# V as the stationary side of the attention's second product, heads normalised in their transposed form

## The reference

```python
def token_mixers(hn, w_in, sink, q_gain, k_gain, rpb, g_grp, w_out):
    proj = jnp.dot(hn, w_in)
    qa, ka, va, qb, kb, vb, qc, kc, vc = jnp.split(proj, offsets, axis=-1)
    ...
    oa = window_sink_attention(...)    # 8 heads, 2 key heads, |q - k| <= 128, a sink logit per head
    ob = dense_block_attention(...)    # 4 heads, 2 key heads, all 512 keys
    oc = neighbourhood_attention(...)  # 4 heads, a 2-D window with a learned bias
    merged = jnp.concatenate([
        rmsnorm(oa, g_grp[:A_WIDTH]),
        rmsnorm(ob, g_grp[A_WIDTH:A_WIDTH + B_WIDTH]),
        rmsnorm(oc, g_grp[A_WIDTH + B_WIDTH:]),
    ], axis=-1)
    return jnp.dot(merged, w_out)

def encoder_layer(x, c, ...):
    hn = rmsnorm(x, g_mix) * (1 + sc1) + sh1
    x = x + gt1 * token_mixers(hn, ...)
    hn = rmsnorm(x, g_ffn) * (1 + sc2) + sh2
    x = x + gt2 * expert_choice_ffn(hn, ...)
    return x
```

## Time and profile before

| | |
|---|---|
| median of 3 runs | 3015.84 us (3008.33 to 3026.54) |
| the profiled execution | 3007.47 us, its span 3005.6 us |
| PE busy in the span | 2685.9 us, 89% |
| weight loads, VectorE, ACT, POOL busy | 54%, 43%, 27%, 9% |
| mean granted clock of TensorE | 0.935 |
| product with V (L1190), 1664 instructions | 231.3 us |
| transposes of the probabilities (L1178), 832 | 144.7 us |

### The profile page before, as it was taken

One profiled execution on the slowest core, in us unless ns is written; L12 is line 12 of the kernel. 1 busy time (PEld: TensorE's weight loads), 2 busy tenths in 40 slices (PEclk: granted clock), 3 DMA queues, 4 the chain that ended last, 5 costly groups with the idle time before them and its releaser, 6 DMA issues.

```text
span 3005.6 us, 32021 instructions
## 1 busy us (share of the span) xinstructions
PE 2685.9 (89%) x10596; PEld 1636.0 (54%) x10596; DVE 1305.8 (43%) x2602; ACT 813.1 (27%) x1613; POOL 269.9 (9%) x260
## 2 busy tenths in 40 slices
PE   6898987989679999999998899698984999999994
PEld 1265764567545555555524567565773555555552
DVE  0346544555434443433404465355554444433444
ACT  0214333154112222222203154232430222222221
POOL 1002000110000000000000110001100000000001
PEclk9898977999789999999999998799996999999997
DMA  9803013021279999999993110213014899999994
GB/s 296 273 1 112 22 43 102 23 90 43 104 246 342 336 353 336 335 335 333 344 315 70 60 60 36 99 25 112 22 43 168 304 353 338 335 336 335 337 341 170
DMA packets 301870, 595.78 MB, mean 198 GB/s; under 512 B 35934, under 2 KB 36078, under 8 KB 301712
## 3 DMA queue, kind: packets, MB, share of 16 engines
q1 hardware_dynamic: 279936, 514.87, 48.1%
q0 software_dynamic: 16976, 62.46, 7.3%
q10 hardware_dynamic: 4832, 16.85, 1.6%
HBM read 552.48 MB, written 43.78 MB: 198 GB/s over the span
## 4 chain that ended last, share of the span: by engine, by line
PE 78%; DVE 8%; issue 7%; DMA 3%; ACT 3%; POOL 1%; POOLq 0%; ACTq 0%; DVEq 0%; SPq 0%; PEld 0%; PEldq 0%
PE bank L1286 29%; PE bank L1139 5%; PE bank L1190 5%; PE bank L1068 4%; PE bank L1303 4%; PE bank L1305 4%; PE bank L1304 4%; PE bank L1169 4%; PE bank L1216 2%; DMA ring<-in_w_ada 2%; PE bank L1178 2%; PE bank L1218 2%; PE bank L1217 2%; PE bank L1236 2%; PE bank L1135 1%
## 5 line engine op out<-in xcount | busy, mean ns | idle before, releaser
L1286 PE MATMUL bank<-ring,hT 128*128 128x512 f32 x2048 | 895.3, 595 | 7.0 <-DVE hT L959 7.0
L1286 PEld LDWEIGHTS bank<-ring,hT 128*128 128x128 f32 x2048 | 388.4, 191 | 473.2 <-issue 470.6
L988 DVE TENSOR_TENSOR ring_r<-ring,down_hi 128x1024 fp32r<-128x1024 f32 x256 | 293.3, 1219 | 0.0
L982 DVE TENSOR_TENSOR pbuf<-pbuf,bank 128x512 f32<-128x512 f32 x64 | 44.0, 688 | 559.2 <-PE bank L1286 559.2
L633 ACT ACTIVATE down_hi<-ring 128x1024 fp32r<-128x1024 f32 x256 | 248.7, 1045 | 99.9 <-DMA ring<-in_w_down 99.9
L1190 PE MATMUL bank<-V,pbuf 128*128 128x64 f32 x1664 | 231.3, 279 | 40.8 <-ACT pbuf L580 30.6
L1190 PEld LDWEIGHTS bank<-V,pbuf 128*128 128x128 f32 x1664 | 215.7, 199 | 59.3 <-ACT pbuf L580 44.5
L1139 PE MATMUL bank<-ring,hT 128*128 128x512 f32 x512 | 228.3, 601 | 0.0
L1303 PE MATMUL bank<-down_hi,hid_hi 128*128 128x512 f32 x512 | 206.5, 403 | 0.0
L1068 PE MATMUL bank<-ring,silu_c 128*2 128x512 f32 x384 | 177.7, 619 | 27.7 <-DMA ring<-in_w_ada 18.2
L1305 PE MATMUL bank<-down_hi,hid_lo 128*128 128x512 f32 x512 | 200.8, 392 | 0.0
(11 more groups left out here) (177 smaller groups left out, 3326.5 us busy)
## 6 DMA issues: line engine op xcount, KB each, us to landing
ring<-in_w_gate SPq DMA_DIRECT2D x64, 2048.0 KB, 10.7
ring<-in_w_up SPq DMA_DIRECT2D x64, 2048.0 KB, 10.1
ring<-in_w_down SPq DMA_DIRECT2D x64, 2048.0 KB, 14.5
ring<-in_w_ada SPq DMA_DIRECT2D x24, 2048.0 KB, 14.7
ring<-in_w_in SPq DMA_DIRECT2D x16, 2048.0 KB, 16.8
ring<-in_w_out SPq DMA_DIRECT2D x8, 2048.0 KB, 10.1
X<-residual ACTq DMA_DIRECT2D x24, 512.0 KB, 3.3
residual<-X POOLq DMA_DIRECT2D x16, 512.0 KB, 2.9
```

What stands on the lines that cost most here:

```text
L988: dve.tensor_tensor(ring_r[4 + n // 4][:, kk:kk + 2, :], ring[4 + n // 4][:, kk:kk + 2, :], full(down_hi[n // 4][kk // 4][:, kk % 4:kk % 4 ...
L1286: ins = pe.matmul(bank[2 * (n % 2) + half][:, :], hT[j % 2][:, k, :], ring[n][:, k, :], start=(k == 0), stop=(k == KT - 1))
```

## The change

The product with V is turned round. V's 64 columns are the stationary side and the transposed probabilities, 128 queries, move. Two heads of a pair (an even and an odd slot) are issued together in the odd slot's turn, one into partitions 0 to 63 and the other into 64 to 127 of bank 5 or 6. The heads thus come out transposed, with features on partitions and queries in columns, in the order of pairs. On the host, the rows of `w_out` and the entries of `g_grp` are put in that order.

The product stands ahead of the transposes of its slot, and it waits for both copies. It waits for `heads_read` at the first pair of each eight heads.

The normalisation works in that form. ACT squares a bank (`heads_a`, `heads_b`). PE sums the squares over the partitions of each head with a two-column constant as moving side (`sum_a`, `sum_b`), which gives one number per query and head. VectorE forms the group's mean with the squared inverse sums; POOL takes the power; VectorE scales the inverse sums (`scale_a`, `scale_b`). PE then spreads each factor over the head's 64 partitions (`spread_a`, `spread_b`), with the factor's column repeated as the stationary side and the identity moving. ACT copies the result out of bank 7, and VectorE multiplies heads, gain and factors in four pieces (`merged_a`, `merged_b`). Rounding and the rest follow as before. All later side steps come two slots later, `normed_0` and `normed_1` three, and the bank's waits count by a table `SIDE`.

```diff
-C_ID, C_MASKA, C_MASKC, C_ROPE, C_END = 0, 128, 512, 576, 1600
+C_ID, C_MASKA, C_MASKC, C_ROPE, C_HALF, C_END = 0, 128, 512, 576, 1600, 1602
...
-AFTER = [(8, "sink"), (8 + V_LAG, "heads_a"), (9 + V_LAG, "scale_a"), (15 + V_LAG, "heads_b"), (17 + V_LAG, "scale_b"),
-         (20, "merged_0"), (21, "split_0"), (22, "merged_1"), (23, "split_1")]
-AFTER += [(23 + 4 * half + quarter, f"out_{half}{quarter}") for half in range(2) for quarter in range(4)]
-AFTER += [(31, "norm"), (32, "normed"), (33, "normed_0"), (34, "normed_1"), (35, "router_0"), (36, "router_1")]
+AFTER = [(8, "sink"), (11, "heads_a"), (17, "sum_a"), (18, "scale_a"), (19, "spread_a"), (20, "merged_a"), (21, "split_a"),
+         (19, "heads_b"), (22, "sum_b"), (23, "scale_b"), (24, "spread_b"), (25, "merged_b"), (26, "split_b")]
+AFTER += [(25 + 4 * half + quarter, f"out_{half}{quarter}") for half in range(2) for quarter in range(4)]
+AFTER += [(33, "norm"), (34, "normed"), (36, "normed_0"), (37, "normed_1"), (37, "router_0"), (38, "router_1")]
 SLOTS = 16 * (TILES - 1) + AFTER[-1][0] + 1
+def heads(p):
+    if p < 4:
+        return slice(p, p + 5, 4)
+    if p < 6:
+        return slice(p + 4, p + 7, 2)
+    return slice(2 * p, 2 * p + 2, 1)
...
+SIDE_ITEMS = ("sum_a", "spread_a", "sum_b", "spread_b", "out_03", "out_13", "normed_0", "normed_1", "router_1")
+SIDE = {}
+for _kind, _i, _k in schedule():
+    if _kind in SIDE_ITEMS:
+        SIDE[_kind, _i] = len(SIDE) + 1
...
                             act.wait_ge(p_turned, m + 1)
                             if m >= 2:
-                                act.wait_ge(pv_done, m - 1)
+                                act.wait_ge(pv_done, m // 2)
                             act.activation(pbuf[:, 3, 0:n], bank[3][:, 0:n], ACT.Copy).then_inc(pt_by_s, 1)
...
-                    if kind in ("merged_0", "merged_1"):
-                        half = int(kind[-1])
-                        act.wait_ge(side_free, 7 * i + 1 + half)
+                    if kind in ("heads_a", "heads_b"):
+                        half = "ab".index(kind[-1])
+                        act.wait_ge(pv_done, 8 * i + 4 * half + 4)
+                        if half:
+                            act.wait_ge(side_full, SIDE["sum_a", i])
+                        elif i:
+                            act.wait_ge(side_full, SIDE["sum_b", i - 1])
+                        act.activation(squares, bank[5 + half][:, :], ACT.Square).then_inc(squared, 1)
+                    if kind in ("spread_a", "spread_b"):
+                        half = "ab".index(kind[-1])
+                        act.wait_ge(side_full, SIDE[kind, i])
                         if i:
-                            act.wait_ge(side_full, 7 * (i - 1) + 4)
+                            act.wait_ge(heads_read, 2 * i - 1 + half)
+                        act.activation(factors[:, 512 * half:512 * half + 512], bank[7][:, :], ACT.Copy).then_inc(spread, 1)
+                        act.wait_ge(spread, 2 * i + half + 1)
+                        act.sem_inc(side_free, 1)
+                    if kind in ("merged_a", "merged_b"):
+                        half = "ab".index(kind[-1])
+                        act.wait_ge(heads_read, 2 * i + half + 1)
+                        if i:
+                            act.wait_ge(side_full, SIDE["out_13", i - 1])
                         part_h = slice(4 * half, 4 * half + 4)
                         act.activation(merged_hi[:, part_h, :], hT[0][:, part_h, :], ACT.Copy).then_inc(merged_hi_ready, 1)
...
-                        a = kind == "heads_a"
-                        half = 0 if a else 1
+                        half = "ab".index(kind[-1])
+                        cols = slice(8 * half, 8 * half + 8)
                         dve.wait_ge(probs_ready, 16 * i + 8 * half + 8)
-                        if a:
+                        if not half:
                             dve.wait_ge(sink_exp, i + 1)
                             chain.add(dve.tensor_tensor(ssum[:, i % 2, 0:8], ssum[:, i % 2, 0:8], stat[:, 16:24], ALU.add))
-                        chain.add(dve.reciprocal(rinv[:, 8 * half:8 * half + 8], ssum[:, i % 2, 8 * half:8 * half + 8]))
-                        dve.wait_ge(pv_done, 16 * i + 8 * half + 8)
-                        if a and i == 0:
-                            dve.wait_ge(gate_turned, 1)
-                        if i and a:
-                            dve.wait_ge(side_full, 7 * (i - 1) + 2)
-                        cols = og[:, 512 * half:512 * half + 512]
-                        dve.tensor_tensor(cols.rearrange("p (h d) -> p h d", d=HD),
-                                          bank[5 + half][:, :].rearrange("p (h d) -> p h d", d=HD),
-                                          bc(rinv[:, 8 * half:8 * half + 8], HD), ALU.mult).then_inc(heads_read, 1)
-                        dve.wait_ge(heads_read, 2 * i + half + 1)
-                        if i and a:
-                            dve.wait_ge(side_full, 7 * (i - 1))
-                        if i and not a:
-                            dve.wait_ge(side_full, 7 * (i - 1) + 4)
-                        junk = hT[1 if a else 0][:, :, :].rearrange("p a b -> p (a b)")
+                        if i:
+                            dve.wait_ge(side_full, SIDE["spread_b" if half else "spread_a", i - 1])
+                        chain.add(dve.reciprocal(rinv[:, cols], ssum[:, i % 2, cols]))
+                        chain.add(dve.tensor_tensor(rinv_sq[:, cols], rinv[:, cols], rinv[:, cols], ALU.mult))
+                    if kind in ("sum_a", "sum_b"):
+                        half = "ab".index(kind[-1])
+                        dve.wait_ge(side_full, SIDE[kind, i])
                         for n, (o, w) in enumerate(GROUP_COLS):
-                            if (o < 512) == a:
-                                ins = dve.tensor_tensor_reduce(junk[:, o:o + w], og[:, o:o + w], og[:, o:o + w], 1.0 / w, EPS,
+                            if (o < 512) != bool(half):
+                                c = slice(o // HD, (o + w) // HD)
+                                ins = dve.tensor_tensor_reduce(soft_junk[:, c], bank[7][:, c], rinv_sq[:, c], 1.0 / w, EPS,
                                                                ALU.mult, ALU.add, stat[:, n:n + 1])
                         ins.then_inc(var_ready, 1)
                         rn[0] += 1
+                        dve.wait_ge(var_ready, rn[0])
+                        dve.sem_inc(side_free, 1)
                     if kind in ("scale_a", "scale_b"):
                         dve.wait_ge(rstd_ready, rn[0])
                         for n, (o, w) in enumerate(GROUP_COLS):
                             if (o < 512) == (kind == "scale_a"):
-                                ins = dve.tensor_scalar(og[:, o:o + w], og[:, o:o + w], stat[:, 8 + n:9 + n], None, ALU.mult)
-                        ins.then_inc(merged, 1)
-                    if kind in ("merged_0", "merged_1"):
-                        half = int(kind[-1])
-                        dve.wait_ge(side_full, 7 * i + 1 + half)
-                        dve.tensor_tensor(hT[0][:, 4 * half:4 * half + 4, :], bank[7][:, :].rearrange("p (a b) -> p a b", a=4),
-                                          bc(rows_t[:, R_GGRP + 4 * half:R_GGRP + 4 * half + 4], P), ALU.mult)\
-                            .then_inc(side_free, 1)
+                                c = slice(o // HD, (o + w) // HD)
+                                ins = dve.tensor_scalar(rinv[:, c], rinv[:, c], stat[:, 8 + n:9 + n], None, ALU.mult)
+                        ins.then_inc(scaled, 1)
+                    if kind in ("merged_a", "merged_b"):
+                        half = "ab".index(kind[-1])
+                        dve.wait_ge(spread, 2 * i + half + 1)
+                        dve.wait_ge(pv_done, 8 * i + 4 * half + 4)
+                        if i:
+                            dve.wait_ge(side_full, SIDE["out_13", i - 1])
+                        for a in range(4):
+                            at = slice(a * P, a * P + P)
+                            ins = dve.scalar_tensor_tensor(out=hT[0][:, 4 * half + a, :], in0=bank[5 + half][:, at],
+                                                           scalar=rows_t[:, R_GGRP + 4 * half + a:R_GGRP + 4 * half + a + 1],
+                                                           in1=factors[:, 512 * half + a * P:512 * half + a * P + P],
+                                                           op0=ALU.mult, op1=ALU.mult)
+                        ins.then_inc(heads_read, 1)
...
+                        m = k - V_LAG
+                        if 0 <= m < UNITS and m % 2 == 1:
+                            _, qp, _, _, _, oc, _ = unit(m % 16)
+                            lo, nb = keys(m // 16, m % 16)
+                            pe.wait_ge(pt_by_s, m // 2 + 1)
+                            pe.wait_ge(pt_by_v, m // 2 + 1)
+                            if m == 9:
+                                pe.wait_ge(gate_ready, 1)
```

(65 more changed lines are left out.)

19 lines of the change are left out of this document (11 added, 8 removed).

## The result

The change makes the kernel slower: 3086.81 us, median of 4 runs (3085.32 to 3091.03), against 3012.09 us (3007.91 to 3026.54, 4 runs) before. The ratio is 1.0237, with an interval of 1.0208 to 1.0266: +75 us by the medians. Between the two profiled executions it is +83.5 us of span (3005.6 to 3089.1).

What follows compares the result with a forecast made beforehand. TensorE bounds most of the span. Per attention -8.2 + 4.5 + 1.9 + 7.3 = +5.5 us, four times +22, plus 10 for clock: 3039.5 profiled, 3048 median; range 2985 to 3128, the forecast's own 3031 to 3065.

Steps and rivals of the forecast that it cites:

- A: Rival: the new waits cost no more than the 3.1 us idle of now, PE's work decides; 2984 us, chance 0.20.
- C: Rival: column halves run one after another; +85 us on the forecast, 3133 us, chance 0.13.
- rival D: Rival: the clock falls for longer, 13 us at half clock in each light stretch; +30, 3078 us, chance 0.12.
- the halves run together: Product with V: two heads' column halves work side by side, a block costs 0.22 us, not 0.42; 5.6 us saved per middle tile.
- the four large ones: PE's idle in tile 2: 1.2 us ahead of spread_a, 1.8 for heads_read, 1.5 at normed_1, 2.3 at router_0.
- B: Rival: half of the waits come, 6 us idle in a full tile at full clock; 3023 us, chance 0.18.
- the forecast of 4.5: Slots 32 to 47 (tile 2) of an attention: 46.0 us becomes 50.5, a loss of 4.5 us.
- slots 0 to 31: First 32 slots of an attention: a gain of 8.2 us, about 62 us where it was 70.6.
- the eleven pairs: Slot pairs before the output products begin: PE's product no longer holds up the next scores; about 0.75 us saved each.
- for each of the eight: Light stretches, eight in all: about 7 us at half clock, 40% busy, adds 1.3 us each, +10 together.
- the light stretch: Slots 33 to 38, where PE is busy under half of 11 us and the clock was expected to fall.
- The tail: Last scores to tile 3's first output product: 22.4 us becomes 30 at half clock, 27 at full; +7.3 taken per attention.

Runs made afterwards that it cites:

- number 10: Changed kernel with the product's two loops swapped, all key blocks of the even head, then of the odd one; 3118.88 us, ratio 1.0335.
- number 3: Changed kernel with identity products added to fill idle PE, into the free scores' bank; 3049.14 us, ratio 1.011.
- number 2: Changed kernel with router_0 one slot later (38, beside router_1); 3046.17 us, ratio 1.0098.
- number 7: number 5 with filling identity products in the tail as well; 3011.16 us, ratio 0.9986.
- number 5: Changed kernel with router_0 one slot later and identity products filling idle PE, none ahead of the router; 3040.3 us, ratio 1.0083.
- 4: Kernel before with both products of a pair issued together ahead of the transposes, V still moving; 3055.65 us, ratio 1.0117.
- number 6: Kernel before with both products of a pair together ahead of the transposes, and router_0 beside router_1; 3017.44 us, ratio 0.9998.
- number 8: Kernel before with filling identity products in slots 0 and 2 and in the tail; 2996.8 us, ratio 0.9933.
- number 9: number 6 with filling products in slots 0 and 2, ahead of normed_0 and in the tail; 2985.43 us, ratio 0.9891.

## Why the prediction was right in its mechanisms and short in its size

The direction held, and 3087 lies in the range of 2985 to 3128. But that range is wide because it takes in parts of A and C; the forecast's own, 3031 to 3065, was missed by 22 us, and that 3087 still lies inside is luck in part: the upper end stood for C, which didn't happen. What happened is nearest to rival D, the clock that falls for longer (3078, given 0.12): the forecast had 56 us more at half clock, D 104, and the traces have 134.

**Right: the halves run together.** Forecast 0.22 per block; measured 0.255, because each group of products has about 0.15 us of start (1.02 for 16 instructions, of which eight pairs at 0.11 are 0.88). Rival C is out. Its price of 83 us for the products was too high as well: in number 10 some overlap remains, and 416 blocks x (0.38 - 0.255) are 52 us, of which 32 show in the time. It confirms that one head after the other would cost about what it cost before, 0.11 an instruction where no halves meet; the saving comes with the alternation. The rule that I had weighed (the Trainium skill, TensorE: Matmul & The Clock Gate, Part 3, loads overlap running products only if their row groups differ) doesn't hold for these column halves, whose row groups are the same: a pair with its loads of 137 ns passes in 0.11 us. The Trainium skill, TensorEngine Tiling (Array Packing), Overview, Theoretical Speedup, gives up to 2x for a dimension of 64 or less; the run shows 1.68 / 1.02 = 1.65.

**Right: the waits.** Three of the four large ones came within 0.25 us of their forecast and the router's within 0.45. Rival A, which needed them to vanish, and B, which needed half, are out. In number 3 the waits and added work of a full tile are +5.4 against the forecast of 4.5.

**Half right: slots 0 to 31.** Eight of the eleven pairs that were to save 0.75 us lie in slots 0 to 15: 28.9 - 6.0 = 22.9. Number 2 has 22.1 there at the full clock; the change has 25.3 at 0.80. The other three pairs should have made slots 16 to 31 39.5; they are 41.2 at the full clock in the first attention and 42.4 to 42.5, with 3.4 us of half clock, in the others, where it was 41.7. The copy's wait is gone there, and PE is busy for 38.2 us where it was 40.7, but the time stayed. Which wait holds the loop instead, no run isolated; that stays open.

**The mis-sized step: "so I add 1.3 us (about 7 us at half clock, 40% busy) for each of the eight: +10".** That is 56 us more at the half clock, at 0.19 us each. The traces have 526 - 392 = 134 us more, and number 3 gives the price: 135 us less of half clock gave 38 us back (the filler's own cost inside), so 0.28 each. Number 7 against number 5 gives 0.25 (29 us for 116), and number 2 without its 14 us of waits 0.34 (27 for 79). The term was about +38, not +10, an estimate from these pairs. Its excess of 28 is more than half of the 51 us by which the spans exceed the forecast. I had put the half clock into the light stretch alone. It also holds in the tile around it (0.85 over 56.2 us is 17 us, none before), in slots 0 to 7 (7 to 11 us in each attention, where two of the four before had none) and in the tail (20 us ahead of the first output product, 8 to 14 before). And I had put it down to waits in general. Numbers 2, 4 and 6 show that one entry of the order, a router that must wait in its slot, starts much of it: taking it away gives 41 us in the turned kernel (14 of them the wait) and 38 in the untransposed one. It isn't the only start, as slots 0 to 7 of three attentions and the tails keep theirs in number 2. Of the other 23 us, slots 16 to 31 are some 7 (41.2 for 39.5, four times), the full tile's waits 4 and the tail's steps 9 (29.2 for 27 near the full clock, four times); the remaining few I can't place.

**The tail: +7.3 forecast, +10.6 as it ran.** The mechanism was right, the steps were priced low: I had 30 us at the half clock and 27 at the full one, and it is 33.0 with 20 of them at the half clock, and 29.2 near the full one (number 7, where number 8 has 20.9). Spreads cost 1.09 and the sum 1.05 where I had 0.9 to 1.0, and at the half clock 1.99 and 1.88. Times four it is +42 for +29.

**What is left for the turned product itself.** With orders and filler matched as well as I could, untransposed and turned are 3017 and 3046 (numbers 6 and 2), and 2985 and 3011 (numbers 9 and 7; their fillers aren't quite the same): turning costs 26 to 29 us. By the starts of the scores in numbers 7 and 9 it gives 2 us in slots 8 to 15 of each attention (12.5 for 14.7) and takes 3 in the full tile (49.5 for 46.3, where each has its least half clock) and about 5 in the tail (52.8 for 47.5). What the change costs is thus some 28 us for turning and some 45 for an order that lets the clock fall, an estimate from those pairs.

## What to carry to other kernels

When an edit moves products together in PE's queue, look at what they had covered: a wait of 1.9 us behind a step that was hidden made its tile 6.7 us longer (number 2), because the clock stayed down after it. Price a light stretch by the tile behind it at the half clock, and try one step a slot later before judging the edit. Where PE must wait anyway, products of no use into a free bank can be cheaper than idling (numbers 3, 7, 8 and 9). Two column halves ran side by side all the way only when their instructions alternated (number 10).

## What the runs showed of the hardware

- Two 64-column halves of the array take a pair of 32-bit passes with 128 moving columns in 0.11 us, loads included (1.02 us for 16 with the start). One half after the other gives 1.51 for the same sixteen.
- A load of 128 columns takes 192 ns for the product before (L1190) and 140 for the transposes (L1178), one of 64 columns for the turned product 137 (L1228). In all three cases an instruction that has no other half beside it takes 0.11 us.
- Added matrix products made the kernel faster four times: 38 us (number 3 against the change), 18 us (number 8 against before), 32 us (number 9 against number 6) and 29 us (number 7 against number 5). The granted clock, as the median of the executions, rose from 0.916 to 0.937, from 0.931 to 0.947, from 0.927 to 0.950 and from 0.935 to 0.953.
- The same four scores take 0.92 us or 1.65 us in one tile, as the clock is 2.4 or 1.2 GHz.
